# A hybrid decoder step on one core: the delta rule's inputs loaded in the first stage, and two groups of cache copies issued from ScalarE

## What is computed

```python
# layer 0
z = h @ w_in
glu = z[..., :D_A] * sigmoid(z[..., D_A:o1])
ca, new_buf_a = causal_dwconv(glu, buf_a, conv_a_w)             # 31 taps
ya = silu(layernorm(ca + conv_a_b, ln_a_g, ln_a_b))
qkv, new_buf_qkv = causal_dwconv(z[..., o1:o2], buf_qkv, conv_qkv_w)   # 4 taps
beta = sigmoid(z[..., o3:o4]); g = -exp(a_log) * softplus(z[..., o4:] + dt_bias)
od, s_new = gated_delta(q, k, v, g, beta, s0)                   # s0 = state_delta
y = concat([ya, rmsnorm(od, gdn_norm_g) * silu(gate)]) @ w_out
# every group of layer 1's caches, 128, 512 and 1024 rows kept
bufs.append(kv_all[:, L + T - keep:])
```

## Time and profile before

| | us |
|---|---|
| median of 3 runs (2545.9 to 2551.32) | 2547.58 |
| the profiled execution, its own time | 2549.36 |
| its span in the profile | 2547.6 |
| PE busy | 2061.0 (81%) |
| VectorE busy | 1281.7 (50%) |
| ScalarE busy | 778.5 (31%) |
| GpSimd busy | 645.0 (25%) |

### The profile page before, as it was taken

The page is one execution under the profiler, slowest core; times in us unless marked ns, Lnnn a source line. Parts: engine busy times, 40 slices in busy tenths (PEclk is TensorE's granted clock), DMA queues, the critical chain, the costliest instruction groups (busy, mean ns, idle before and its releaser), DMA issues. The chain is left out here.

```text
span 2547.6 us, 25620 instructions
## 1 busy us (share of the span) xinstructions
PE 2061.0 (81%) x9026; PEld 1031.3 (40%) x9026; DVE 1281.7 (50%) x3157; ACT 778.5 (31%) x2275; POOL 645.0 (25%) x645
## 2 busy tenths in 40 slices
PE   7893797478787898877699999987888887988766
PEld 5682685243222243322244464554532222432222
DVE  0084643264677667775511031123556677666754
ACT  1141100024444344443411122121234444344443
POOL 0000000034443444434201000000344434454341
PEclk9985766789999999998799999999899999999978
DMA  5894999679999999999938755753899999999995
GB/s 196 306 339 137 335 331 332 236 268 405 427 427 427 427 427 414 427 426 427 411 147 335 276 200 206 284 199 125 338 426 426 427 427 427 426 423 427 427 427 243
DMA packets 129427, 874.97 MB, mean 343 GB/s; under 512 B 15876, under 2 KB 29700, under 8 KB 45195
## 3 DMA queue, kind: packets, MB, share of 16 engines
q0 software_dynamic: 92160, 662.74, 62.6%
q1 hardware_dynamic: 37139, 210.60, 23.4%
HBM read 861.98 MB, written 118.81 MB: 385 GB/s over the span
## 5 line engine op out<-in xcount | busy, mean ns | idle before, releaser
L1430 PE MATMUL tail_acc<-tail_ring,tail_diag 128*128 128x512 f32 x1216 | 597.7, 622 | 111.5 <-ACT tail_diag L1289 110.6
L1177 DVE CUSTOM_DVE_ANT_0 tail_ring<-tail_ring,all_h 128x1024 f32<-128x1024 f32 x344 | 418.8, 1223 | 235.8 <-DMA tail_ring<-in_peer_uv,tail_idx 235.3
L1430 PE MATMUL tail_acc<-mid_wring,tail_diag 128*128 128x512 f32 x832 | 413.3, 624 | 98.7 <-ACT tail_diag L1289 98.5
L1570 POOL DMA_INDIRECT mid_wring<-in_peer_uv,tail_idx x232 | 239.0, 1030 | 1001.7 <-DVE all_x L1062 525.8
L1570 POOL DMA_INDIRECT tail_ring<-in_peer_uv,tail_idx x344 | 369.4, 1074 | 480.4 <-PE tail_acc L1430 410.8
L1430 PEld LDWEIGHTS tail_acc<-tail_ring,tail_diag 128*128 128x128 f32 x1216 | 217.0, 193 | 477.2 <-ACT tail_diag L1289 297.3
L1177 DVE CUSTOM_DVE_ANT_0 mid_wring<-mid_wring,all_h 128x1024 f32<-128x1024 f32 x232 | 283.3, 1223 | 175.4 <-DMA mid_wring<-in_peer_uv,tail_idx 174.1
L1283 ACT ACTIVATE tail_gelus<-tail_dots 128x1 f32<-128x1 f32 x576 | 116.2, 202 | 723.3 <-DVE tail_dots L1177 723.0
L1430 PEld LDWEIGHTS tail_acc<-mid_wring,tail_diag 128*128 128x128 f32 x832 | 147.8, 193 | 352.6 <-ACT tail_diag L1289 223.9
L1681 PE MATMUL mix_acc<-mid_wring,all_hT 128*128 128x512 f32 x576 | 273.4, 610 | 1.5 <-PEq L80 1.4
L1289 ACT ACTIVATE tail_diag<-all_ident,tail_weights 128x128 f32<-128x128 f32 x512 | 205.5, 401 | 26.4 <-PE tail_acc L1430 9.9
(11 more groups left out here) (363 smaller groups left out, 2099.3 us busy)
## 6 DMA issues: line engine op xcount, KB each, us to landing
mid_wring<-in_w_qkv SPq DMA_DIRECT2D x18, 2048.0 KB, 8.8
out_kv_s<-in_cache_kv_w SPq DMA_DIRECT2D x8, 4064.0 KB, 49.2
mix_ring<-in_kT POOLq DMA_DIRECT2D x16, 1024.0 KB, 8.1
mix_ring<-in_v_rows POOLq DMA_DIRECT2D x16, 1024.0 KB, 10.3
ab_ring_w<-in_w_in_ab SPq DMA_DIRECT2D x6, 2048.0 KB, 11.4
mix_ring<-in_kT POOLq DMA_DIRECT2D x16, 768.0 KB, 9.3
mix_ring<-in_v_rows POOLq DMA_DIRECT2D x16, 768.0 KB, 9.0
mid_wring<-in_w_out SPq DMA_DIRECT2D x4, 2048.0 KB, 10.4
```

What stands on the lines that cost most here:

```text
L1177: V.tensor_tensor_reduce(out=u, in0=u, in1=h[:, g, :], scale=1.0, scalar=0.0, op0=ALU.mult, op1=ALU.add, accum_out=dots[:, n:n + 1]).then_ ...
L1430: last = mm(acc[g][:, c * 512:(c + 1) * 512], diag[:, n % DIAGS, :], v[:, c * 512:(c + 1) * 512], start=first, stop=final)
L1570: pool.indirect_dma_start(slot(r), None, table, bass.IndirectOffsetOnAxis(ap=idx[:, j, i:i + 1], axis=0)).then_inc(landed[r], 16)
```

## The change

The fourteen loads of the delta stage are made into a list by `delta_inputs`, whose tiles now live through the whole of layer 0 (they are called l_ instead of gd_), and SP issues them in the first stage behind the three weight chunks. The six copies of group 1 in the convolution stage and the eight of group 2 in the delta stage are issued by ScalarE, ahead of its first activation of the stage, instead of by SP. Nothing else is changed.

```diff
--- before.py
+++ after.py
@@ -147,7 +147,7 @@
 
 
 
-def first_norm_phase(nc, K, T, hT, ahead):
+def first_norm_phase(nc, K, T, hT, ahead, later):
 
     x, xs, h, hs = K["x"], K["xs"], K["h"], K["hs"]
     with ExitStack() as ctx:
@@ -166,6 +166,8 @@
                 sp.dma_start(gain[:], broadcast_rows(T["norm_mix"][0:1, :], D)).then_inc(gain_in, 16)
                 sp.dma_start(gain_s[:], T["gain_s"][0]).then_inc(gain_in, 16)
                 for to, frm, landed in ahead:
+                    sp.dma_start(to, frm).then_inc(landed, 16)
+                for to, frm, landed in later:
                     sp.dma_start(to, frm).then_inc(landed, 16)
 
             @block.vector
@@ -447,7 +449,6 @@
                 sp.dma_start(rq[24:28, :], T["conv_qkv_w"][0]).then_inc(loaded, 16)
 
                 sp.dma_start(T["out_conv_a_s"][0, :, 0:26, :], T["state_conv_a"][0, :, 4:30, :]).then_inc(stored, 16)
-                roll_cache(sp, T, 1, cache_out, range(2, DEC_B))
                 sp.wait_ge(tail_copied, 4)
                 sp.dma_start(T["out_conv_a_p"][0, 0], tail_a[0:30, :]).then_inc(stored, 16)
                 sp.dma_start(T["out_conv_qkv_p"][0, 0], tail_q[0:3, :]).then_inc(stored, 16)
@@ -529,6 +530,7 @@
 
             @block.scalar
             def _(act):
+                roll_cache(act, T, 1, cache_out, range(2, DEC_B))
                 nc.scalar.activation(zT[:, 4:8, :], zT[:, 4:8, :], ACT.Sigmoid).then_inc(sig_ready, 1)
                 for r in range(4):
                     act.wait_ge(tail_ready, r + 1)
@@ -566,7 +568,22 @@
 
 
 
-def delta_phase(nc, name, K, T, hT, zT, conv, mixT, cache_out):
+def delta_inputs(P, T):
+
+    G = {"cst": P.sb("masks", [128, 12, 128]), "own": P.sb("owner", [128, DEC_B]), "wab": P.sb("w_ab", [128, KC, 8]),
+         "alog": P.sb("a_log", [128, 4]), "dtb": P.sb("dt_bias", [128, 4]), "gn": P.sb("norm_gain", [128, 1]),
+         "S0": P.sb("S_sample", [128, DEC_B, 4, 128])}
+    loaded = P.sem("delta_loaded")
+    loads = [(G["wab"][:], T["w_in_ab"][0].rearrange("(k p) n -> p k n", p=128)[:, :, IN_AB - 8:IN_AB], loaded),
+             (G["cst"][:], T["c_gdn"].rearrange("p (k n) -> p k n", k=12), loaded),
+             (G["own"][:], T["c_owner"], loaded), (G["alog"][:], broadcast_rows(T["a_log"], 4), loaded),
+             (G["dtb"][:], broadcast_rows(T["dt_bias"], 4), loaded),
+             (G["gn"][:], T["gdn_norm_g"].rearrange("a n -> n a"), loaded)]
+    loads += [(G["S0"][:, b, :, :], T["state_delta"][0, b].rearrange("h k v -> k h v"), loaded) for b in range(DEC_B)]
+    return G, loaded, loads
+
+
+def delta_phase(nc, name, K, T, G, loaded, hT, zT, conv, mixT, cache_out):
 
 
 
@@ -601,10 +618,7 @@
 
     with ExitStack() as ctx:
         P = Phase(nc, ctx, name)
-        cst = P.sb("masks", [128, 12, 128])
-        own = P.sb("owner", [128, DEC_B])
-        wab = P.sb("w_ab", [128, KC, 8])
-        alog, dtb, gn = P.sb("a_log", [128, 4]), P.sb("dt_bias", [128, 4]), P.sb("norm_gain", [128, 1])
+        cst, own, wab, alog, dtb, gn, S0 = (G[k] for k in ("cst", "own", "wab", "alog", "dtb", "gn", "S0"))
         ab, gt = P.sb("ab", [128, 3, 8]), P.sb("g_tmp", [128, 3, 4])
         beta, g = P.sb("beta", [128, 3, 4]), P.sb("g", [128, 3, 4])
         per_tile = lambda name, shape: [P.sb(f"{name}{t}", shape) for t in range(3)]
@@ -618,12 +632,11 @@
         Rv, Rk, kd = per_tile("Rv", [128, 4, 128]), per_tile("Rk", [128, 4, 128]), P.sb("k_decay", [128, 3, 4, 128])
         u, wT, qe = P.sb("u", [128, 3, 4, 128]), P.sb("wT", [128, 3, 4, 128]), P.sb("q_exp", [128, 3, 4, 128])
         S, vn, vs = P.sb("S", [128, 4, 128]), P.sb("v_new", [128, 4, 128]), P.sb("v_new_s", [NS, 4, 128])
-        S0 = P.sb("S_sample", [128, DEC_B, 4, 128])
         wS, vm = P.sb("wS", [128, 4, 32]), P.sb("v_owner", [32, DEC_B, 128])
         oT, ones = P.sb("oT", [128, 4, NTOK]), P.sb("ones", [128, 128])
         sqr = P.sb("sqr", [128, 4, NTOK])
         bank = [P.ps(f"bank{i}", [128, 512]) for i in range(8)]
-        loaded, dve_steps, act_steps, stored = (P.sem(s) for s in ("loaded", "dve_steps", "act_steps", "stored"))
+        dve_steps, act_steps, stored = (P.sem(s) for s in ("dve_steps", "act_steps", "stored"))
         turn = {"gates": P.sem("gate_turn"), "main": P.sem("main_turn")}
         turn.update({t: P.sem(f"tile{t}_turn") for t in range(3)})
         heads = [b[:].rearrange("q (h c) -> q h c", h=4) for b in bank]
@@ -654,17 +667,6 @@
         with nc.Block() as block:
             @block.sync
             def _(sp):
-                sp.dma_start(wab[:], T["w_in_ab"][0].rearrange("(k p) n -> p k n", p=128)[:, :, IN_AB - 8:IN_AB]
-                             ).then_inc(loaded, 16)
-                sp.dma_start(cst[:], T["c_gdn"].rearrange("p (k n) -> p k n", k=12)).then_inc(loaded, 16)
-                sp.dma_start(own[:], T["c_owner"]).then_inc(loaded, 16)
-                sp.dma_start(alog[:], broadcast_rows(T["a_log"], 4)).then_inc(loaded, 16)
-                sp.dma_start(dtb[:], broadcast_rows(T["dt_bias"], 4)).then_inc(loaded, 16)
-                sp.dma_start(gn[:], T["gdn_norm_g"].rearrange("a n -> n a")).then_inc(loaded, 16)
-                for b in range(DEC_B):
-                    sp.dma_start(S0[:, b, :, :], T["state_delta"][0, b].rearrange("h k v -> k h v")
-                                 ).then_inc(loaded, 16)
-                roll_cache(sp, T, 2, cache_out)
                 sp.wait_ge(turn["main"], at["main", "c3 S dve"] + 1)
                 sp.dma_start(T["out_delta_p"][0, 0].rearrange("h k v -> k h v"), S[:]).then_inc(stored, 16)
                 sp.wait_ge(turn[2], len(order[2]))
@@ -783,6 +785,7 @@
             def _(act):
                 ch = Chain(act, act_steps)
                 A = nc.scalar.activation
+                roll_cache(act, T, 2, cache_out)
                 begin(act, "gates", "ab act")
                 ch.step(A(beta[:], ab[:, :, 0:4], ACT.Sigmoid))
                 ch.step(A(alog[:], alog[:], ACT.Exp))
@@ -2244,17 +2247,18 @@
 
         with ExitStack() as c2:
             P0 = Phase(nc, c2, "l0")
+            G, delta_loaded, delta_loads = delta_inputs(P0, T)
             zT, conv = P0.sb("zT", [128, 24, NTOK]), P0.sb("conv", [128, 12, NTOK])
             with ExitStack() as c3:
                 W = WeightRing(Phase(nc, c3, "ab_ring"), T["w_in_ab"][0], IN_AB - 8, 3)
-                first_norm_phase(nc, K, T, hT, W.start)
+                first_norm_phase(nc, K, T, hT, W.start, delta_loads)
                 def copies(sp):
                     roll_cache(sp, T, 0, cache_out)
                     roll_cache(sp, T, 1, cache_out, range(2))
 
                 columns_phase(nc, "ab", hT, T["w_in_ab"][0], IN_AB - 8, zT, ahead=W, after=copies)
             conv_phase(nc, "cv", K, T, zT, mixT, conv, cache_out)
-            delta_phase(nc, "gd", K, T, hT, zT, conv, mixT, cache_out)
+            delta_phase(nc, "gd", K, T, G, delta_loaded, hT, zT, conv, mixT, cache_out)
 
         with ExitStack() as c2:
             P1 = Phase(nc, c2, "mid")
```

## The result

The changed kernel takes 2631.76 us (median of 4 runs, 2627.23 to 2635.09) against 2546.74 us of the kernel before in the same comparison (4 runs): ratio 1.0331, 95% interval 1.0314 to 1.0348, so 85 us or 3.3% slower. The profiled execution took 2630.64 us, its span is 2628.8 us, 81.2 us over that of before.

A forecast was written before the change was run, and what follows sets the result against it. It took DMA to be full nearly throughout, with PE waiting for late loads and stores ending the delta stage. +16.3 + 69 - 11 = +74.3 us gave 2623.7 for a like run, about 2622 against the median; range 2574 to 2642.

The forecast's parts named there:

- Part 1: First stage: fourteen delta loads behind the weights stall SP's issue ahead of the barrier, +16.3 us (bounds +5.9 to +20).
- Part 2: Convolution stage: loads take turns with ScalarE's six copies and land at 200 instead of 130.9, +69 us (+60 to +74).
- step of turns: Convolution stage's DMA: queues alternate one packet each whatever its size, so each small load packet lets a 3.13 us one go first.
- last step: Convolution stage: some engines get more than the average 19 load rows, since 31, 3 and 24 rows do not spread evenly.
- cap: Convolution stage: no engine is held longer than the copies last, 24 large packets each, ending at about 201 as before.
- The same work as after 131.07, 108 us: Convolution stage after the loads land: VectorE and PE do unchanged work, 108 us to the stage's end.
- Part 3: Delta stage: PE starts 14.0 us earlier, but stores end the stage at 451 instead of 462.17, -11 us (-9.8 to -16.6).
- B: Rival, convolution stage: a turn passes a whole transfer's share on an engine, +25 us there, 2578 in all; chance 0.12.
- C: Rival, convolution stage: both issuers feed one line in order of issue, sum +52 us, 2600; chance 0.10.
- D: Rival: SP's queue is served ahead of ScalarE's, convolution loads land as before, delta stage gives 16.6 us; 2547 or 2537; chance 0.07.
- A: The main forecast, all three parts as predicted, 2606 to 2640 us; chance 0.64.
- E: Rival worse than A: convolution loads held past 200 us, or first stage at its upper bound, 2640 to 2665; chance 0.07.

The follow-up runs named there:

- the second experiment: The kernel before with only the convolution stage's six copies moved from SyncE to ScalarE: 2623.29 us, ratio 1.0291.

## Why the prediction was right, point by point

**Part 1, +16.3 us for the first stage.** Right in that SP's issue stalls ahead of the barrier, which its issue times of 4.85 and 5.00 us show, 14.5 measured; it was done at 34.85, not 36.8. The term was 1.8 us too large. By the packets of SP's queue some 2,490 were issued and not yet started when the first of these two issues ended, and some 1,610 when the second did, against my 1,700 to 2,500. The eight states were not held: their issue took 6.33 us, 6.57 in the earlier trace rows. That a full queue is what stalls SP is an estimate of mine; the runs show the stalls, and no one number of packets at which they end. By the packets the weights end at 29.6 and the added loads at 38.2, so they took 8.6 us back to back and not 10.5. What was left when SP's last issue ended fits the forecast:

```profile
DMA packets 1806, 0.89 MB, mean 88 GB/s; under 512 B 62, under 2 KB 1806, under 8 KB 1806
```

These are the packets started from 34.85 to 45 us, 1,744 of them rows of loads, where I had taken 1,727. That nothing covers it was shown by the move to the projection stage.

**Part 2, +69 us of wait.** That the loads passed ahead of the copies in the kernel before is in its packets, from 117.7 to 124.4 and from 124.4 to 131 us:

```profile
DMA packets 32, 2.08 MB, mean 311 GB/s; under 512 B 0, under 2 KB 0, under 8 KB 0
...
DMA packets 405, 2.60 MB, mean 394 GB/s; under 512 B 72, under 2 KB 72, under 8 KB 374
```

The 32 are rows of older copies, 65,024 bytes each; the last 16 of them end between 124.8 and 126.3 us. The 302 rows of the loads all start from 124.8 to 130.3, half of them by 126.5. In the kernel after, q10 moves ScalarE's six copies in 384 packets of 65,024 bytes, one for each row, at 3.05 us of an engine each. The step of turns was right: 79 and 79 packets, and the wait follows the length of the rows (89.14 us with these, 61.58 with rows of 16,256 bytes). Measured was 74.3 (PE 87.7 us after the stage's start instead of 13.4), just past the upper bound of 74. What I had under-sized was the last step, "a few rows more than 19" on some engines. One engine had all 31 rows of the taps (the run with them in two transfers took 23.3 us off the wait), so it was held as long as it had copies, and its last rows moved only from 217.7 us on, 84 us after the stage's start. The cap was the second error: I took the copies to end at about 201 on every engine, and in the kernel before the last of their rows ends at 207.7. From the stage's start that is 90.0 us, and 88.7 in the kernel after. "The same work as after 131.07, 108 us" was not met either: from PE's start to the stage's end it took 104.0 us. The part in which PE has the diagonal matmuls, in the kernel before:

```profile
140.00:195.40 55.40, 55.05 (x316) 50.15 (x316) 48.91 (x175) 28.72 (x88) 0.00 (x0) 0.94 0.99 328
...
253.30:437.60 184.30, 152.01 (x824) 132.64 (x824) 88.17 (x219) 9.97 (x20) 0.00 (x0) 0.66 1.00 335
```

The first row stands against 230 to 282 of the kernel after: the same 316 matmuls were busy for 51.68 instead of 55.05 us, at a granted clock of 1.00 instead of 0.94. The two errors nearly cancel, and that is luck: the stage is 70.3 us longer. Nor can the 4 us be put down to the long wait. With a wait of 90.37 us and the copies on ScalarE (the second experiment) the same part took 106.2 us, with waits of 13 to 15 us 105.7 to 108.1, and with 61.58 us 109.3. It was shorter where PE's matmuls were busy for less time (71.2 us in all in the kernel after, 76.9 in the one before, 78.1 in the last named), but what sets that isn't settled by these runs.

**Part 3, -11 us.** Measured -9.6. PE's start was 14 us earlier within the stage, as forecast, and VectorE's end even 19.4 (219.8 and 200.4 us after the stage's start), since from PE's start to the last state the stage took 178.7 instead of 184.3 us, with PE busy for 148.17 instead of 152.01 us for the same 824 matmuls. In all eight profiles with early loads this part took 177.8 to 178.7 us, in the two with loads in the stage 184.3 and 182.1; why isn't shown. None of it counted, because the stores ended the stage, 13.0 us after VectorE. I had forecast 6 us of this wait. The copies' last row ended 205.3 us after the stage's start instead of 215.1, so only the 9.8 us by which they were issued earlier came back, my lower bound, and not 11. That the stores wait for the copies whichever queue they are in was shown by the two variants with and without ScalarE's queue: in both, as in the kernels before and after, the last row of the stores starts 6.7 to 6.8 us after the copies' last row ends.

**What follows.** "Only shifted" held within the spread: from the start of the next stage to the end the ten profiles of this study have 2083.4 to 2090.3 us, the kernels before and after 2085.4 and 2090.3. The 4.9 us between them are not put down to the change.

**The rivals.** B (a turn by transfer) and C (one line in order of issue) fell with the run of 16 KB rows and with q10. D (SP's queue first) fell with the wait of 89.14 us. The sum for a like run, 2623.7, was 6.9 us below the profiled 2630.64: 5.3 us too little in the wait of Part 2, 1.4 in Part 3, 1.1 in the projection and 4.9 in what follows, against 1.8 too much in Part 1 and 4.0 in the rest of the convolution stage. The other 2.9 us to the median of 2631.76 lie in how the profiled runs stand to their medians. The range held, with its upper part: the 2606 to 2640 given for A aren't what the bounds of the three parts add to, which is 49.3 to 84.2 us or 2597 to 2632, and the measured 2631.76 lies at the very end of that. The 119.5 in the sum of Part 2 comes from no row either; from the stage's start at 117.70 with the backlog of 7 us doubled it's 117.70 + 14 + 59 = 191, the same. E's reason, loads held past 200 us by engines that carry both, is in part what came: counted from the stage's start they were held to what would have been 205.4.

## What to carry to other kernels

In these runs SP's and ScalarE's queues share the DMA engines by taking turns of one packet (79 and 79 packets in 15 us), so a transfer that somebody waits for must not stand in one queue while another holds long rows: count its rows on the fullest engine, times what a row of the other queue takes there (3.05 us for 65,024 bytes, 0.77 us for 16,256). Issued ahead of the copies in the same queue it is protected by the order of issue (14.78 us of wait instead of 89.14), and issuing the long copies only when the loads have landed does the same (15.32 us). Load early, but from a stage in which the issuing engine has time to spare: issues that stalled ahead of the first stage's barrier cost all engines 14.5 us, and the same loads issued behind it nothing that can be seen. And where a stage ends with stores, spread the copies ahead of them so that they are nearly drained by then (9.02 us for the issue of the eight stores instead of 28.56).
